# The keys' projections of a two-layer encoder by seven block products, with the norm's row multiplied in once per unit

## The reference

```python
# layer 0
h = rmsnorm(x, norm_mix[0])
proj = h @ w_in                                  # 1024 x 3072
qa, ka, va, qb, kb, vb = jnp.split(proj, ...)    # six parts of 512 columns
# differential attention on qa, ka, va; neighbourhood attention on qb, kb, vb
x = x + concat(o_a, o_b) @ w_out
# layer 1
h = rmsnorm(x, norm_mix[1])
proj = h @ w_in                                  # q 512, k 512, v 1024, g 1024, gf 16, gb 16
# log gates from gf, gb; chunked gated linear attention in both directions on q, k, v
o = rmsnorm(o, out_norm) * silu(g)
x = x + o @ w_out
# each layer ends with a mixture of 32 experts:
x = x + hierarchical_moe(rmsnorm(x, norm_ffn[layer]), ...)
```

## Time and profile before

| | |
|---|---|
| median of 3 runs | 1170.35 us (1170.03 to 1171.16) |
| profiled execution | time 1171.89 us, span 1170.0 us |
| TensorE busy | 985.1 us, 84% of the span |
| weight loads | 478.9 us, 41% |
| VectorE, ScalarE, GpSimd busy | 311.7, 133.2, 65.7 us |
| DMA | 442.44 MB, 378 GB/s in the mean |
| mean granted TensorE clock | 0.933 of full |

### The profile page before, as it was taken

How to read it: one execution, slowest core, us unless ns; L and a number is a source line. 1 busy time by engine, 2 the same in 40 slices (tenths; PEclk the granted TensorE clock), 3 DMA queues, 4 the chain that set the end, 5 groups by cost and what they waited for, 6 DMA issues and landing times.

```text
span 1170.0 us, 13097 instructions
## 1 busy us (share of the span) xinstructions
PE 985.1 (84%) x5388; PEld 478.9 (41%) x5388; DVE 311.7 (27%) x689; ACT 133.2 (11%) x324; POOL 65.7 (6%) x40
## 2 busy tenths in 40 slices
PE   9999999967777677987999999999767767778866
PEld 8875653323213223342488766433132132232422
DVE  2365352201101101130354763522111111112203
ACT  2124010000000000000132221000000000000002
POOL 3100000000000000000082300000000000000000
PEclk9999999989879989988999999999899898799888
DMA  9925989999999999999993547899999999999996
GB/s 371 413 85 213 416 312 421 425 427 428 427 429 429 428 429 425 429 425 423 412 391 144 216 176 327 309 422 429 427 428 427 428 429 427 429 427 426 425 422 251
DMA packets 40162, 442.44 MB, mean 378 GB/s; under 512 B 4482, under 2 KB 4866, under 8 KB 13092
## 3 DMA queue, kind: packets, MB, share of 16 engines
q1 hardware_dynamic: 39956, 441.48, 90.5%
q10 hardware_dynamic: 144, 0.12, 0.0%
HBM read 440.53 MB, written 1.05 MB: 377 GB/s over the span
## 4 chain that ended last, share of the span: by engine, by line
PE 55%; DMA 36%; DVE 3%; SPq 3%; issue 2%; ACT 1%; DVEq 0%; POOL 0%; POOLq 0%
PE psum L1956 53%; DMA sb_weights<-moe_w_down 31%; DMA sb_weights<-moe_w_gate 5%; SPq L731 2%; SPq L737 1%; PE psum L2619 1%; DVE sb_weights L1815 1%; PE psum L2199 0%; DVE sb_hT L1203 0%; PE psum L2487 0%; DVE sb_x L1835 0%; ACT sb_weights L1100 0%; PE psum L1994 0%; DVE sb_small L1168 0%; PE psum L1967 0%
## 5 line engine op out<-in xcount | busy, mean ns | idle before, releaser
L1956 PE MATMUL psum<-sb_weights,sb_hT 128*32 128x512 f32 (+3 forms) x2312 | 422.5, 612 | 102.4 <-DMA sb_weights<-moe_w_gate 59.8
L1956 PE MATMUL psum<-sb_weights 128*32 128x512 f32 (+10 forms) x1784 | 351.8, 543 | 41.4 <-DMA sb_weights<-moe_w_down 35.3
L1956 PEld LDWEIGHTS psum<-sb_weights,sb_hT 128*32 128x32 f32 (+2 forms) x2312 | 140.4, 127 | 360.8 <-issue 278.5
L1956 PEld LDWEIGHTS psum<-sb_weights 128*32 128x32 f32 (+5 forms) x1784 | 143.2, 142 | 233.3 <-issue 186.0
L1828 DVE TENSOR_TENSOR sb_hn<-sb_hn,psum 128x512 f32<-128x512 f32 x72 | 49.4, 686 | 223.7 <-PE psum L1956 223.5
L1956 PE MATMUL psum<-sb_hT,sb_weights 128*128 128x256 f32 (+1 forms) x400 | 88.8, 380 | 0.6 <-DVE sb_hT L1203 0.5
L1956 PEld LDWEIGHTS psum<-sb_hT,sb_weights 128*128 128x128 f32 (+1 forms) x400 | 74.0, 187 | 12.8 <-issue 1.1
L1956 PE MATMUL psum<-sb_weights,sb_x 128*128 128x192 f32 (+2 forms) x448 | 72.1, 320 | 6.4 <-issue 5.7
L1956 PEld LDWEIGHTS psum<-sb_weights,sb_x 128*128 128x128 f32 x448 | 69.1, 203 | 11.1 <-issue 9.9
L1820 DVE COPY sb_weights<-psum 96x512 f32<-96x512 f32 (+1 forms) x20 | 13.7, 686 | 178.5 <-PE psum L1956 178.5
L1815 DVE TENSOR_TENSOR sb_weights<-sb_weights,psum 96x512 f32<-96x512 f32 (+1 forms) x22 | 15.0, 683 | 151.6 <-PE psum L1956 151.6
(11 more groups left out here) (230 smaller groups left out, 470.2 us busy)
## 6 DMA issues: line engine op xcount, KB each, us to landing
sb_weights<-moe_w_gate SPq DMA_DIRECT2D x58, 2048.0 KB, 24.6
sb_weights<-moe_w_down SPq DMA_DIRECT2D x58, 2048.0 KB, 27.0
sb_weights<-moe_w_up SPq DMA_DIRECT2D x48, 2048.0 KB, 27.1
sb_weights<-moe_w_up SPq DMA_DIRECT2D x22, 1024.0 KB, 19.8
sb_weights<-moe_w_gate SPq DMA_DIRECT2D x24, 512.0 KB, 7.1
sb_weights<-od_w_in_units SPq DMA_DIRECT2D x6, 2048.0 KB, 27.3
sb_weights<-ev_w_in_units SPq DMA_DIRECT2D x5, 2048.0 KB, 25.1
sb_weights<-moe_w_up SPq DMA_DIRECT2D x16, 512.0 KB, 10.4
```

The lines of the kernel that those rows point to most:

```text
L1956: return nc.tensor.matmul(o, l, r, start=start, stop=stop, skip_group_check=True)
```

## The change

Unit 1 of both layers, the keys, joins the units by blocks, as entries w = 0 and w = 2. Their result is wanted with columns on partitions, so they are computed turned: the stationary operand is a 128x128 block of weights (or of a sum of weights), the streamed one 128 tokens, and a product is 8 calls of 128 columns. The parts are copied without a scale, the four result blocks are plain additions, and when the fourth is copied the whole of the keys, 128x1024, is multiplied by inv_row in place. The scratch for the new sums is a free stretch of the arena in layer 0 and hn in layer 1. The entries after them are renumbered (GATES 3 becomes 5), with their counts and waits.

```diff
-        BY_BLOCKS = ((0, 2), (1, 2), (1, 3), (1, 4), (1, 5))
-        GATES = 3
-        BLOCK_BANKS = ((2, 0), (0, 1), (1, 0), (0, 1), (1, 0))
-        SUM_MADE = (dict(t2=6, t3=7, t4=8), dict(t2=14, t3=15, t4=23), dict(t2=17, t3=18, t4=24),
-                    dict(t3=19, t2=20, t1=25, t4=26), dict(t3=21, t2=22, t1=27, t4=28))
+        BY_BLOCKS = ((0, 1), (0, 2), (1, 1), (1, 2), (1, 3), (1, 4), (1, 5))
+        TURNED = (0, 2)
+        GATES = 5
+        BLOCK_BANKS = ((3, 1), (2, 0), (0, 1), (1, 0), (0, 1), (1, 0), (0, 1))
+        SUM_MADE = (dict(t2=6, t3=7, t4=11), dict(t2=9, t3=10, t4=12),
+                    dict(t2=18, t3=19, t4=23), dict(t2=21, t3=22, t4=31), dict(t2=25, t3=26, t4=32),
+                    dict(t3=27, t2=28, t1=33, t4=34), dict(t3=29, t2=30, t1=35, t4=36))
...
+        def turned_block(c, kh, n):
+            return unit[c].rearrange("p (b k m) -> p b k m", b=4, k=2)[:, 2 * n:2 * n + 2, kh]
...
             sum_rows(0, 0)
             sum_weights(0)
+            sum_weights(1)
             sum_last(0)
+            sum_last(1)
...
-                    sum_rows(1, 8)
-                    for w in (1, 2):
-                        sum_weights(w)
-                    for w in (3, 4):
-                        sum_gates(w)
-                    for w in (1, 2):
-                        sum_last(w)
-                    for w in (3, 4):
-                        sum_gates_last(w)
+                    sum_rows(1, 12)
+                    sum_weights(2)
+                    sum_weights(3)
+                    sum_last(2)
+                    sum_weights(4)
+                    sum_gates(5)
+                    sum_gates(6)
+                    sum_last(3)
+                    sum_last(4)
+                    sum_gates_last(5)
+                    sum_gates_last(6)
...
+                if w in TURNED:
+                    nc.scalar.activation(part(w, i), bank, ACT.Copy).then_inc(part_read, 1)
...
+                for i in range(3):
+                    take_part(2, i)
                 for h in range(C_HEADS):
                     act.wait_ge(cum_psum, h + 1)
...
+            def turned_piece(w, i):
+                layer = BY_BLOCKS[w][0]
+                t, n = ((0, 0), (1, 1), (0, 1), (1, 0))[i]
+                bank = psum[:, BLOCK_BANKS[w][(1, 0, 1, 0)[i]], 0:SEQ].rearrange("p (b t) -> p b t", b=2)
+                ts = slice(t * P, (t + 1) * P)
+                dst = kT[:, 2 * n:2 * n + 2, ts] if layer else qkT[:, 4 + 2 * n:6 + 2 * n, ts]
+                if i < 3:
+                    dve.wait_ge(product_psum, 6 * w + (2, 5, 6)[i])
+                    dve.wait_ge(part_read, 3 * w + (1, 3, 2)[i])
+                    other = part(w, (0, 2, 1)[i]).rearrange("p (b t) -> p b t", b=2)
+                    nc.vector.tensor_tensor(dst, bank, other, ALU.add).then_inc(block_done, 1)
+                else:
+                    dve.wait_ge(proj_psum, 2 * IN_UNITS * layer + 2 * BY_BLOCKS[w][1] + 2)
+                    nc.vector.tensor_copy(dst, bank).then_inc(block_done, 1)
+                    dve.wait_ge(block_done, blocks_before(w) + 4)
+                    keys = kT if layer else qkT[:, 4:8, :]
+                    chained(nc.vector.tensor_tensor(keys, keys, inv_row[layer].unsqueeze(1).to_broadcast([P, 4, SEQ]), ALU.mult))
...
                     nc.vector.tensor_tensor(lg[:, c], lg[:, c], lgtmp[:, c], ALU.subtract).then_inc(lg_done, 1)
-                projected(2)
-                projected(3)
-
-                take_block(1, 0)
+                for i in range(4):
+                    take_block(2, i)
+                take_block(3, 0)
...
+                    if w in TURNED:
+                        for nb in range(2):
+                            for j in range(4):
+                                ins = mm(psum[:, bank, nb * P:(nb + 1) * P], weights[:, nb, j * P:(j + 1) * P], rows[:, j],
+                                         start and nb == j == 0, j == 3)
+                        return ins
...
-                for g in range(4):
+                for g in range(2):
                     project0(g, 0)
                     if g == 0:
                         spread_inverse(0)
                     project0(g, 1)
                 project_by_blocks(0)
+                project_by_blocks(1)
...
-                for g in range(1, 4):
-                    project1(g, 0)
-                    project1(g, 1)
+                project1(1, 0)
+                project1(1, 1)
+                project_by_blocks(2)
...
-                for w in (1, 2):
+                for w in (3, 4):
                     project_by_blocks(w)
```

More of the change, by code:

```diff
@@ L553, in part @@
         def part(w, i):
-            return parts[(0, 1, 1, 2, 2)[w]][:, i * SEQ:(i + 1) * SEQ]
+            return parts[(0, 0, 1, 1, 1, 2, 2)[w]][:, i * SEQ:(i + 1) * SEQ]
         PROJ_UNITS = 12
@@ L794, in sum_weights @@
                 layer, c = BY_BLOCKS[w]
-                b11, b12, b21, b22 = (weight_block(c, kh, n) for kh in range(2) for n in range(2))
+                block = turned_block if w in TURNED else weight_block
+                b11, b12, b21, b22 = (block(c, kh, n) for kh in range(2) for n in range(2))
                 t1, t2 = (weight_sum(w, i) for i in range(2))
                 gp.wait_ge(in_full[c], 16 * (layer + 1))
+                if w == 2:
+                    gp.wait_ge(inv_done, 4)
                 made(gp.tensor_tensor(t1, b12, b11, ALU.subtract), SUM_MADE[w]["t2"] - 1)
@@ L933, in mixer0 @@
                                          ACT.Copy).then_inc(hTc_done, 1)
-                for i in range(3):
-                    take_part(0, i)
+                for w in range(2):
+                    for i in range(3):
+                        take_part(w, i)
                 act.wait_ge(lam_sum, 1)
@@ L1273, in mixer0 @@
                 chained(nc.vector.tensor_scalar(inv_row_q, inv_row[0], B_DH ** -0.5, None, ALU.mult))
-                for i in range(4):
+                for i in range(2):
                     projected(i)
-                for i in range(4):
-                    take_block(0, i)
+                for w in range(2):
+                    for i in range(4):
+                        take_block(w, i)
                 dve.wait_ge(tables_loaded, 3 * 16)
@@ L1477, in mixer1 @@
                 for i in range(1, 4):
-                    take_block(1, i)
-                take_block(2, 0)
+                    take_block(3, i)
+                take_block(4, 0)
                 decayed(1)
@@ L1482, in mixer1 @@
                 for i in range(1, 4):
-                    take_block(2, i)
+                    take_block(4, i)
                 decayed(3)
@@ L1554, in mixer1 @@
                 masked(0)
-                take_block(3, 0)
+                take_block(5, 0)
                 states(0, 0)
@@ L1558, in mixer1 @@
                 masked(1)
-                take_block(3, 1)
-                take_block(3, 2)
+                take_block(5, 1)
+                take_block(5, 2)
                 states(0, 2)
@@ L1564, in mixer1 @@
                 states(1, 1)
-                take_block(4, 0)
+                take_block(6, 0)
                 states(1, 2)
@@ L1571, in mixer1 @@
                 states(2, 2)
-                take_block(4, 1)
+                take_block(6, 1)
                 gated(1)
                 states(3, 0)
-                take_block(4, 2)
+                take_block(6, 2)
                 states(3, 1)
@@ L2083, in block_product @@
                     if w < 2:
[L2084 to L2085 removed]
+                        pe.wait_ge(proj0_done, 2 - w)
+                    elif w == 2:
+                        pe.wait_ge(proj1_done, 2)
+                    elif w < 6:
                         pe.wait_ge(block_done, before)
@@ L2092, in block_product @@
                     pe.wait_ge(block_sums, made["t2"])
-                    product(first, row_sum(layer, 1), lambda j: sum_column(w, j), False).then_inc(product_psum, 1)
+                    product(first, row_sum(layer, 1), summed(1), False).then_inc(product_psum, 1)
                 elif i == 3:
@@ L2097, in block_product @@
                         pe.wait_ge(block_sums, made["t1"])
-                    weights = block(0, 0) if w >= GATES else lambda j: weight_sum(w, 0)[:, j]
-                    product(second, row_sum(layer, 0), weights, True).then_inc(product_psum, 1)
+                    product(second, row_sum(layer, 0), block(0, 0) if w >= GATES else summed(0), True).then_inc(product_psum, 1)
                 elif i == 4:
```

116 lines of the change are left out of this document (63 added, 53 removed).

## The result

| | before | after |
|---|---|---|
| median of 20 runs | 1170.60 us (1169.82 to 1173.11) | 1172.89 us (1169.82 to 1175.13) |
| profiled execution: time, span | 1171.89, 1170.0 us | 1172.14, 1170.3 us |
| mean granted clock | 0.933 | 0.937 |

The ratio is 1.0014, 95% interval 1.0008 to 1.0021: slower by 1.6 us (0.9 to 2.5). The prediction said 1169.9, a little faster; the median lies outside its range.

The account below looks back on a forecast made before the run. TensorE was taken to bound the two mixers, weight loads the expert rounds. Layer 0's -0.7 us and layer 1's +0.3 us sum to -0.4 us, from a median of 1170.35 to 1169.9 us; range 1167.6 to 1172.4.

Parts of the forecast that it names:

- I let a shift pass in full: In both mixers: each microsecond TensorE's order of work gains or loses there goes to the end of the kernel.
- everything after it moves along: In a mixer, TensorE events restart the DMA queue, so all later work shifts with them.
- The price of a narrow product: Keys' units on TensorE: 112 records of 128 columns at 0.1116 us, 12.5 us a unit, gaining 1.32 us, twice.
- The rival in which loads and products add up: Keys' units: weight loads do not hide, 0.227 us a record, 25.5 us a unit, 1193 us total; chance 0.03.
- Layer 0's wait: TensorE waits 0.6 us for GpSimd's last sum before the keys' seventh product; net gain 0.7 us.
- Layer 1's stall: TensorE stands before unit 2's seventh product, 0.4 to 2.0 us, taken as 1.6; net +0.3 us.
- no waits: Layer 1: VectorE's small operations need not take turns with GpSimd, so no waits behind the sums; 1168.3 us, chance 0.25.
- the hole closes: Layer 1: the fourth subtraction meets GpSimd's seventh sum, delaying the keys' fourth product, +2.0 us, 1171.9; chance 0.13.
- The rival of an unseen wait: A wait not seen in the hand-written order of three engines; 1172.5 to 1176 us, chance 0.05.

Follow-up runs that it names:

- e9: Changed kernel plus 128 long-satisfied TensorE waits (64 instructions) in layer 0's unit 0, no other edit; median 1171.16 us, ratio to before 0.9992.
- e15: Kernel before plus waits making exactly 98 more TensorE instructions ahead of layer 0's first quarter release; median 1174.36 us, ratio 1.0026.
- e13: Kernel before plus long-satisfied waits making 65 more TensorE instructions in layer 0; median 1170.50 us, ratio 0.9998.
- e11: Changed kernel with GpSimd's sums reordered in both layers, plus 128 long-satisfied TensorE waits in layer 0; median 1167.57 us, ratio to before 0.9967.
- e8: Kernel before with only layer 1's keys by blocks and GpSimd's order mended there; median 1169.22 us, ratio 0.9984.
- e1: Changed kernel with GpSimd's sums reordered and gate sums held back, so neither predicted TensorE wait is left; median 1170.70 us, ratio to before 0.9998.
- e10: Kernel before plus 98 long-satisfied TensorE waits in layer 0, which made only 36 instructions; median 1171.94 us, ratio 0.9999.
- e12: e8 plus 98 long-satisfied TensorE waits in layer 0, which made only 36 instructions; median 1170.37 us, ratio to before 0.9989.
- e6: Kernel before with one 0.43 us call in layer 0's unit 2 made three times, to end its mixer later; median 1171.19 us, ratio 1.0000.

## Why the prediction was wrong

- **What failed** is the sentence "I let a shift pass in full", and "everything after it moves along" before it. The 0.49 us that layer 0 gained did not pass: it became +1.40 by the second round of experts. The runs put in its place: the change also moved a fetch of instructions onto the issue of the first quarter matrices, their load slows (1.1 us lost in bytes), and the round after it waits for them. Taken away (e9), the same kernel keeps its lead to 272 us (-0.85 to -0.89; at 602.7 us -0.41 is left of it, which is not traced), and its ratio is 0.9992 (0.9982 to 1.0002), where -0.4 us would be 0.9997. Put into the kernel before (e15), it costs 0.26% (0.16 to 0.37); the same kernel with 33 instructions fewer (e13) stands at 0.9998.
- **A shift passes where no such packet meddles.** e11: -1.48 at 65.6, 222.9 and 272.5 us; e8: the 1.3 us of layer 1 arrive at the end.
- **The price of a narrow product** held: the 96 records from 22.94 on follow each other every 0.1116 us, and the keys' unit of layer 1, which has no wait, goes from 604.15 to 616.65: 12.50 us, as worked out. The rival in which loads and products add up (25.5 us a unit, 1193 in all) fell. That was what the prediction made of a rule of the Trainium skill. The rule stands in "TensorE: Matmul & The Clock Gate" under "The mechanism", not under the heading that the prediction names, and the same section also lets a weight load run ahead into a background weight buffer. The trace does not agree with the rule taken alone: these 112 records came every 0.1116 us, loads and all. Which buffer the loads used it doesn't show.
- **Layer 0's wait**: 0.6 worked out, 0.65 measured from start to start; net 0.49 instead of 0.7. The unit 0 before it started 0.10 us later (12.58 for 12.48), and the 16 records after the wait took 0.07 us more than at 0.1116 each: -1.32 + 0.10 + 0.65 + 0.07 = -0.50.
- **Layer 1's stall**: 1.6 taken, 1.47 measured from start to start, released by VectorE; both copies in one gap was the 1.4 of the prediction. The 24 records after it took another 0.11 us. Net +0.27, against +0.3. e1 confirms the cause: with the sums in another order the stall is gone. The rivals "no waits" and "the hole closes" fell: the subtractions ended at 607.5, before GpSimd's sum at 608.03.
- **The rival of an unseen wait** (chance 0.05, 1172.5 to 1176) just covers the measured 1172.9, and by luck: it looked in the order of three engines, and the wait lay some 120 us behind the edit, for loads that a queue disturbs of which the prediction shows no row.

## What to carry to other kernels

An edit that changes how many instructions an engine executes moves every later fetch of its code. Look where the instruction packets of the DMA trace stand against the first issue of a burst of loads, above all where the kernel goes from computing to loading; if one stands there, some satisfied waits ahead of it move it away. Here that was worth 2.6 and 3.6 us by the ratios (e9, e11), where the edit itself was forecast to give 0.4. And compare issue times row by row, and bytes moved up to one moment: two spans that agree within 0.3 us held a loss of 1.9 and a gain of 1.5 at other places.

## What the runs showed that was not expected

- The Trainium skill's "mostly hidden" does not hold for the packet at 155.9 us; what the other 41 of the changed kernel cost was not measured one by one. A packet of 16 KB, 7.2% of the 16 DMA engines over 0.8 us, goes with 1.0 to 1.5 us of loads lost when it starts within 0.1 us of the first issue after the DMA engines stood idle (five profiles), and with 0.2 us or less when it starts 0.6 us before or earlier, or 5.8 us after or later (thirteen profiles).
- Why so small a transfer should cost so much stays open in part. The issue that waits for the packet's end accounts for 0.5 to 0.7 us. An issue drawn out in the same way while the DMA engines are full costs nothing (e11 at 214.87 us, 1.40 us long, its lead unchanged at 1.46). Why the loads after it run at 158 to 279 GB/s (160 to 162 us, the five profiles) instead of 385 for some 6 us, with the DMA share at 0.59 (e15) to 0.94 (changed kernel), no run here shows.
- e10 falls back 1.7 us at 272 us and has it back at 316; e10 and e12 both fall back about 1 us between 449 and 559 us. Whether other packets do that was not tried.
- VectorE's operations with two SBUF inputs took turns with GpSimd's sums as before (1.29 us for two of 128x512 when GpSimd is idle, 5.50 beside its sums), and a sum that met the multiplication of 128x1024 took 3.22 instead of 2.35 us.
- The granted clock of a stretch of 10 to 20 us falls to 0.83, 0.84 or 0.91 in single executions, in either layer, and 1.5 us goes each time. It came at 720 to 740 us in the profiles of before, e1, e9 and e15, and at 150 to 160 us in those of e6 and e15; no edit explains it.
